# Splitting a sum of squares in high and low halves on VectorE, and two fp32r products in place of one in fp32, in the state-space rounds

## The chip, the cores and the metric

The kernel runs on one core of one Trainium2 chip. The time is that of one execution on the device, in microseconds; a run's time is compared as the median of several. All tensors are fp32 in memory. TensorE multiplies either in fp32 or in fp32r, a format that keeps fewer bits of each number. The kernel makes up for that by splitting operands in a high half (the value rounded to fp32r) and a low half (what is left of it).

## What is computed

Two transformer-like blocks in a row on 256 tokens of width 1024. The change lies in the second block, in its state-space branch (Mamba-2). There, 2048 channels stand in 8 groups of 256, and the result of each group is gated and then normed over the group's 256 channels:

```python
y = ssd_chunked(xh, dt, a, bm, cm)
y = y + d_skip.reshape(SSM_GROUPS, hg)[:, :, None] * xh
y = y.reshape(b, s, SSM_INNER) * jax.nn.silu(z)
yg = y.reshape(b, s, SSM_GROUPS, SSM_INNER // SSM_GROUPS)
yg = yg * lax.rsqrt(jnp.mean(yg * yg, axis=-1, keepdims=True) + RMS_EPS)
y = yg.reshape(b, s, SSM_INNER) * norm_w
```

The sum of `yg * yg` over the 256 channels of a group is what the change computes in another way.

## The kernel before

**Units.** All large products read weights in units of 1024 by 256. SyncE loads a unit into `raw`, ScalarE copies it to fp32r (`split_hi`, line 208, into `w_hi`), VectorE subtracts that from the raw values (`split_lo`, line 214, into `w_lo`), and TensorE makes three products of each 128-row slice (`products`, line 246: high by high, high by low, low by high). There are three slots for units, and a bank of PSUM for each. A slot is filled again once its unit is done; a bank once VectorE or ScalarE has evacuated it.

**Rounds.** The eight groups are worked on in rounds. In round i (1 to 7), TensorE runs the unit `x` of group i, `ssm_scores(i-1)`, the first half of the unit `b_c`, `ssm_sums(i-2)`, the second half, `ssm_values(i-1)` and the unit `z` (lines 2034 to 2043). Each engine has its order written out by hand, and takes its instructions in that order; between engines, semaphores hold them apart.

VectorE in round i (lines 1526 to 1539): `ssm_inputs(i-1)` (lines 1466 and 1468, waits for the scores), a weight split, `ssm_mask(i-1)` (line 1477, waits for ScalarE's decay; `ssm_values(i-1)` on TensorE waits for it), `ssm_scale(i-2)` (line 1509, waits for the norm), `ssm_low(i-2)` (line 999, waits for ScalarE's `ssm_out`), `ssm_skip(i-1)` (1484), an evacuation (989), a weight split, the convolution (1205), a weight split, `ssm_gate(i-1)` (1491 and 1493) and `ssm_pair(i-1)` (1498).

ScalarE in round i (lines 902 to 917): evacuation of `x` (459), a weight copy, four convolution taps (611), a weight copy, the exponents (860), the silu (848), a weight copy, `ssm_square(i-1)` (873), the silu of `z`, the decay (868), `ssm_norm(i-1)` and `ssm_out(i-1)` (lines 449, 450 and 883). The norm waits for TensorE's `ssm_sums(i-1)`, which stands in TensorE's round i+1.

**The sum of squares.** ScalarE squares the gated result of a group, `d_y`, two tiles of 128 channels by 256 tokens, into `d_sq`. VectorE adds the two tiles (`ssm_pair`, line 1498). TensorE multiplies the sum by a matrix of ones in fp32 (`ssm_sums`, line 2024, through the helper `mm`, line 1637), which adds over the 128 partitions. ScalarE turns the result into the inverse root (`ssm_norm`), and VectorE scales `d_y` by it (`ssm_scale`).

**After the rounds** (lines 2045 to 2056): the gate units `ga`. Their first bank is freed by ScalarE's `gate` (line 694), which stands behind `ssm_out(6)` in ScalarE's order. `ssm_pair(7)` and `ssm_sums(7)` lie among these units.

`Chain` (line 86) is a helper: called with an instruction, it lets it raise a semaphore and makes the same engine wait for that before its next instruction. `x_hi` and `x_lo` are the fp32r operand tiles, `OPND` = 40 of them each of 128 by 256; in the rounds the last two are free.

Of the kernel before, what the change touches and what calls it, by code (L numbers as in the profile page):

```python
# [8 lines left out]
FP32 = mybir.dt.float32  # L9
FP32R = mybir.dt.float32r  # L10
ALU = mybir.AluOpType
ACT = mybir.ActivationFunctionType
AXX = mybir.AxisListType.X

P = 128
T = 256
# [43 lines left out]
OPND = 40  # L60
# [37 lines left out]
def build(nc, a, out):  # L98

    ctx = ExitStack()  # L100
    with ctx:
        def sb(name, shape, dt=FP32):
            return ctx.enter_context(nc.sbuf_tensor(name, shape, dt))
# [3 lines left out]
        def S(name):  # L107
            if name not in sems:
                sems[name] = ctx.enter_context(nc.semaphore(name))
            return sems[name]  # L110
# [6 lines left out]
        x_hi = sb("x_hi", [P, OPND, T], FP32R)  # L117
        x_lo = sb("x_lo", [P, OPND, T], FP32R)
# [3 lines left out]
        ident, ones, later = (cst[:, n * P:(n + 1) * P] for n in range(3))  # L122
# [15 lines left out]
        def cells(at, *dims):  # L138
            n = 1
            for d in dims:  # L140
                n *= d
            v = arena[:, at:at + n]
            if len(dims) == 2:
                return v.rearrange("p (a b) -> p a b", a=dims[0])
            if len(dims) == 3:
                return v.rearrange("p (a b c) -> p a b c", a=dims[0], b=dims[1])
            return v

        def bank(b, *dims):
            v = ps[:, b, :]  # L150
            if len(dims) == 3:
                return v[:, 0:dims[0] * dims[1] * dims[2]].rearrange("p (a b c) -> p a b c", a=dims[0], b=dims[1])
            if len(dims) == 2:
                return v[:, 0:dims[0] * dims[1]].rearrange("p (a b) -> p a b", a=dims[0])
            return v[:, 0:dims[0]]
# [8 lines left out]
        def need(eng, name, n):  # L164

            if n > 0:
# [10 lines left out]
        n_hi, n_lo = (v[:, M0:M0 + 3, :].rearrange("p a b -> p (a b)").rearrange("p (h c) -> p h c", h=2)  # L177
                      for v in (x_hi, x_lo))
        ones_r, later_r = (x_hi[:, M0 + 3, n * P:(n + 1) * P] for n in range(2))
        dtc, acs = (small[:, n:n + 64].rearrange("p (t h) -> p t h", t=2) for n in (256, 320))  # L180
        skip = tab[:, 40 * KT:40 * KT + 16]
        dtb, a_log = (tab[0:32, n:n + 1] for n in (40 * KT + 16, 40 * KT + 17))
# [67 lines left out]
        def thin_products(dst, hi, lo, at):  # L250

            for k in range(KT):
                for m, (wt, xt) in enumerate(((hi, x_hi), (hi, x_lo), (lo, x_hi))):
# [25 lines left out]
        d_ab, d_cb, d_xd, d_ec, d_sq, d_r, d_y = (cells(3584, 4, T), cells(4624, 384), cells(5008, 2, T), cells(5520, 4, 384),  # L279
                                                  cells(2576, 2, T), cells(3088, T), cells(7056, 2, T))  # L280
# [34 lines left out]
        def U(stage, i, n=0, per=1):  # L315
            return BASE[stage] + per * i + n
# [125 lines left out]
        def _(act):  # L442
            ahead = iter(range(len(FILLED)))
            chain = Chain(act, S("act_chain"))
            A = nc.scalar.activation
# [6 lines left out]
            def tables():  # L452

                act.preload_act_table_set("natural_log_exp_and_others")  # L454

            def evac(u, dst, func=ACT.Copy):

                finished(act, u)
                A(dst, unit_bank(u), func).then_inc(taken(u), 1)

            def split():

                split_hi(act, next(ahead))
# [374 lines left out]
            def ssm_tap(i):  # L838

                evacuated(act, U("ssm", i, 0, 3))  # L840
                evacuated(act, U("ssm", i, 1, 3))
                need(act, "d_L", i)
                first_tap(d_xp, d_cv, "_2", ssm_tiles(i)).then_inc(S("rnn_c0"), 1)

            def ssm_silu(i):

                act.wait_ge(S("rnn_cv"), i + 5)
                A(d_cv, d_cv, ACT.Silu).then_inc(S("rnn_qk"), 1)  # L848

            def ssm_z(i):  # L850

                evac(U("ssm", i, 2, 3), d_z, ACT.Silu)

            def ssm_exponents(j, heads=range(4)):

                act.wait_ge(S("rnn_bc"), 16 * j + 80)
                act.wait_ge(S("rnn_num"), j + 4)
                for h in heads:
                    for s, (lo, hi, at) in enumerate(((0, T, 0), (P, T, T))):
                        last = A(decay(j)[:, h, at:at + hi - lo], d_ab[:, h, lo:hi], ACT.Relu,  # L860
                                 bias=acs[:, s, 4 * j + h:4 * j + h + 1], scale=-1.0)
                if 3 in heads:
                    last.then_inc(S("rnn_e"), 1)

            def ssm_decay(j):

                act.wait_ge(S("rnn_e"), j + 5)
                A(decay(j), decay(j), ACT.Exp, scale=-1.0).then_inc(S("rnn_w"), 1)

            def ssm_square(j):  # L870

                act.wait_ge(S("rnn_hm"), j + 5)
                A(d_sq, d_y, ACT.Square).then_inc(S("rnn_sq"), 1)

            def ssm_norm(j):

                act.wait_ge(S("rnn_ss"), j + 5)
                inv_rms(d_r, bank(6, T), T).then_inc(S("rnn_r"), 1)

            def ssm_out(j):  # L880

                act.wait_ge(S("rnn_y"), j + 5)
                A(rows(x_hi, 2 * j + YSS, 2), d_y, ACT.Copy).then_inc(S("y_hi"), 1)
# [15 lines left out]
            tables()  # L899
            ssm_decay(0)  # L900

            for i in range(1, 8):
                evac(U("ssm", i, 0, 3), d_xp[:, 0:2, 3:259])
                split()
                ssm_tap(i)
                split()
                ssm_exponents(i)
                ssm_silu(i)
                split()
                ssm_square(i - 1)  # L910
                ssm_z(i)
                tables()
                ssm_decay(i)
                if i == 7:
                    split()
                ssm_norm(i - 1)
                ssm_out(i - 1)
# [58 lines left out]
        def _(dve):  # L976
            ahead = iter(range(len(FILLED)))
            chain = Chain(dve, S("dve_chain"))
            V = nc.vector
            tt, ts, stt = V.tensor_tensor, V.tensor_scalar, V.scalar_tensor_tensor  # L980
# [29 lines left out]
            for b in range(4):  # L1010
                v = slice(2 * b, 2 * b + 2)
# [483 lines left out]
            def ssm_pair(j):  # L1495

                dve.wait_ge(S("rnn_sq"), j + 5)
                tt(d_sq[:, 0], d_sq[:, 0], d_sq[:, 1], ALU.add).then_inc(S("d_pair"), 1)

            def ssm_conv(i):  # L1500

# [120 lines left out]
            for t in range(2):  # L1622
# [3 lines left out]
                for h in range(2):  # L1626
                    v = y_cols(h)
# [5 lines left out]
        def _(pe):  # L1633
            FP, TOK = False, True

            def mm(o, l, r, start=True, stop=True):
                return nc.tensor.matmul(o, l, r, start=start, stop=stop)  # L1637
# [58 lines left out]
            k, q, v = cross_units(0)  # L1696
# [68 lines left out]
            for i in range(1, 5):  # L1765
                k, q, v = (U("cross", i, n, 3) for n in range(3))
# [49 lines left out]
            for i in range(1, 4):  # L1816
                q, k, v = (U("stick", i, n, 3) for n in range(3))
# [36 lines left out]
            q, k, v, o = (U("mlstm", 0, n, 4) for n in range(4))  # L1854
# [8 lines left out]
            for i in range(1, 4):  # L1863
                q, k, v, o = (U("mlstm", i, n, 4) for n in range(4))
# [112 lines left out]
            q, k, v = (U("att", 0, n, 3) for n in range(3))  # L1977
# [8 lines left out]
            for i in (1, 2):  # L1986
                q, k, v = (U("att", i, n, 3) for n in range(3))
# [32 lines left out]

            def ssm_sums(j):

                pe.wait_ge(S("d_pair"), j + 1)
                mm(bank(6, T), ones, d_sq[:, 0]).then_inc(S("rnn_ss"), 1)

            x, b_c, z = (U("ssm", 0, n, 3) for n in range(3))
            att_logits(2)
# [182 lines left out]
```

## Time and profile before

| what | value |
|---|---|
| time, median of 3 runs (range) | 1212.14 us (1210.88 to 1213.48) |
| the profiled execution's own time | 1213.69 us |
| its span | 1211.9 us |
| TensorE busy | 1195.8 us (99%), 9406 products |
| VectorE busy | 819.0 us (68%) |
| ScalarE busy | 672.0 us (55%) |
| mean granted clock of TensorE | 0.996 |

The state-space rounds lie between about 740 and 900 us of the span. Engines are named PE (TensorE products), PEld (TensorE weight loads), DVE (VectorE), ACT (ScalarE). Durations of products overlap, since they are pipelined; their cost is read from one start to the next. An fp32 product is listed as two records.

### The profile page before, as it was taken

The page shows a single profiled execution, that of the slowest core. Times are in us where ns is not written, and L with a number is a line of the kernel's source. Part 1 is how long each engine was busy: PE and PEld are TensorE (multiplying, and loading weights), DVE is VectorE, ACT ScalarE, POOL GpSimd, SP SyncE. Part 2 cuts the span into 40 slices and gives each one's busy share as a digit, 9 for nine tenths or more (in the row PEclk, how much of TensorE's full clock was granted, in tenths as well). Part 3 has the DMA queues.
Part 4 walks back from the last instruction along what each step waited for, and adds up shares of the span by engine and source line. Part 5 has one row for each costly group of instructions (what it writes and reads, how often), then busy time and mean ns, then how long its engine had stood idle before and what let it go on. Part 6 is the DMA issues. An engine that isn't in the chain of part 4 may idle for free.

```text
span 1211.9 us, 21581 instructions
## 1 busy us (share of the span) xinstructions
PE 1195.8 (99%) x9406; PEld 1163.3 (96%) x9406; DVE 819.0 (68%) x928; ACT 672.0 (55%) x802; POOL 11.0 (1%) x24
## 2 busy tenths in 40 slices
PE   9999999999999999999999999999999999999998
PEld 8999999999999999999999998999999998999886
DVE  7866677777655557776547757899985457777543
ACT  7643645676553455544435548889876345555442
POOL 0000000000000000000000000000000000000000
PEclk9999999999999999999999999999999999999999
DMA  9553545555555554556565546556555664455651
GB/s 326 169 162 106 167 146 148 148 150 175 184 194 180 179 168 151 194 184 210 174 206 178 183 133 182 173 160 198 156 164 172 195 208 142 155 174 183 234 191 52
DMA packets 202493, 210.73 MB, mean 174 GB/s; under 512 B 6540, under 2 KB 191244, under 8 KB 202400
## 3 DMA queue, kind: packets, MB, share of 16 engines
q1 hardware_dynamic: 199712, 200.30, 52.1%
q0 software_dynamic: 2112, 8.17, 2.3%
q8 instruction: 74, 1.21, 0.5%
q10 hardware_dynamic: 576, 0.90, 0.2%
q14 instruction: 19, 0.16, 0.0%
HBM read 208.25 MB, written 1.09 MB: 173 GB/s over the span
## 4 chain that ended last, share of the span: by engine, by line
PE 80%; DVE 12%; ACT 5%; issue 1%; DMA 1%; DVEq 0%; ACTq 0%
PE ps L246 64%; PE ps L2128 7%; DVE w_lo L214 5%; PE ps L1637 4%; DVE arena L1205 3%; ACT w_hi L208 2%; PE ps L1686 1%; DVE arena L1477 1%; PE ps L2088 1%; PE ps L1640 1%; DMA arena<-rows 1%; DVE arena L1509 0%; PE ps L254 0%; ACT L454 0%; DMA pcol<-in_params 0%
## 5 line engine op out<-in xcount | busy, mean ns | idle before, releaser
L246 PE MATMUL ps<-x_hi,w_hi 128*128 128x256 f32 x2448 | 701.9, 287 | 1.9 <-ACT arena L694 1.4
L246 PE MATMUL ps<-x_hi,w_lo 128*128 128x256 f32 x2448 | 692.9, 283 | 0.0
L246 PE MATMUL ps<-x_lo,w_hi 128*128 128x256 f32 x2448 | 692.9, 283 | 0.0
L214 DVE TENSOR_TENSOR w_lo<-raw,w_hi 128x2048 fp32r<-128x2048 f32 x187 | 427.5, 2290 | 227.1 <-ACT w_hi L208 227.1
L246 PEld LDWEIGHTS ps<-x_hi,w_hi 128*128 128x128 f32 x2448 | 469.9, 192 | 6.4 <-issue 3.7
L246 PEld LDWEIGHTS ps<-x_lo,w_hi 128*128 128x128 f32 x2448 | 470.0, 192 | 0.7
L246 PEld LDWEIGHTS ps<-x_hi,w_lo 128*128 128x128 f32 x2448 | 469.8, 192 | 0.0
L208 ACT CAST w_hi<-raw 128x2048 fp32r<-128x2048 f32 x187 | 354.3, 1900 | 115.4 <-PE ps L246 71.2
L1637 PE MATMUL ps<-arena 128*128 128x256 f32 (+5 forms) x432 | 66.0, 340 | 0.9 <-ACT arena L848 0.7
L246 PE MATMUL ps<-w_hi,x_hi 128*128 128x256 f32 x224 | 64.3, 287 | 0.0
L246 PE MATMUL ps<-w_lo,x_hi 128*128 128x256 f32 x224 | 63.3, 283 | 0.0
L246 PE MATMUL ps<-w_hi,x_lo 128*128 128x256 f32 x224 | 63.3, 283 | 0.0
L1205 DVE SCALAR_TENSOR_TENSOR arena<-arena,pcol 128x256 f32<-128x256 f32 x144 | 60.1, 480 | 3.5 <-ACT arena L611 2.7
L768 ACT ACTIVATE arena<-ps 128x512 f32<-128x512 f32 x30 | 17.9, 598 | 77.6 <-PE ps L246 77.6
L1637 PEld LDWEIGHTS ps<-arena 128*128 128x128 f32 (+2 forms) x432 | 52.9, 170 | 8.3 <-ACT arena L848 0.9
L2128 PE MATMUL ps<-w_hi,x_hi 128*128 128x512 f32 x128 | 49.8, 389 | 0.0
L2128 PE MATMUL ps<-w_hi,x_lo 128*128 128x512 f32 x128 | 49.8, 389 | 0.0
L2128 PE MATMUL ps<-w_lo,x_hi 128*128 128x512 f32 x128 | 49.8, 389 | 0.0
L1367 DVE TENSOR_TENSOR arena<-arena 128x512 f32<-128x512 f32 x32 | 22.1, 692 | 32.0 <-ACT arena L768 32.0
L246 PEld LDWEIGHTS ps<-w_hi,x_lo 128*128 128x128 f32 x224 | 42.9, 191 | 0.0
L246 PEld LDWEIGHTS ps<-w_hi,x_hi 128*128 128x128 f32 x224 | 42.9, 191 | 0.0
L246 PEld LDWEIGHTS ps<-w_lo,x_hi 128*128 128x128 f32 x224 | 42.9, 191 | 0.0
(237 smaller groups left out, 945.3 us busy)
## 6 DMA issues: line engine op xcount, KB each, us to landing
raw<-in_w_in SPq DMA_DIRECT2D x170, 512.0 KB, 4.7
raw<-in_w_ff SPq DMA_DIRECT2D x64, 512.0 KB, 4.5
raw<-in_w_up SPq DMA_DIRECT2D x32, 512.0 KB, 4.7
raw<-in_w_down SPq DMA_DIRECT2D x32, 512.0 KB, 4.6
raw<-in_w_mem_kv SPq DMA_DIRECT2D x16, 512.0 KB, 6.1
raw<-in_w_out SPq DMA_DIRECT2D x16, 512.0 KB, 4.4
raw<-in_w_ssm_proj SPq DMA_DIRECT2D x16, 512.0 KB, 4.6
raw<-in_w_x_proj SPq DMA_DIRECT2D x8, 512.0 KB, 4.4
```

The lines of the kernel that those rows point to most:

```text
L208: nc.scalar.copy(w_hi[:, s], raw[:, s]).then_inc(S(f"w_hi{s}"), 1)
L214: nc.vector.tensor_tensor(w_lo[:, s], raw[:, s], w_hi[:, s].bitcast(FP32), ALU.subtract)\
L246: last = nc.tensor.matmul(dst, l, r, start=start and k == 0 and m == 0, stop=stop and k == nk - 1 and m == 2)
L768: A(f, unit_bank(u), ACT.Relu).then_inc(taken(u), 1)
L1205: last = stt(dst[:, n], pad[:, n, m:m + T], pc("conv_w" + name, tiles[n] + stride * m), dst[:, n], ALU.mult, ALU.add)
L1367: chain(tt(q, f, bc(rs_row(), 2), ALU.mult))
L1477: tt(decay(j), decay(j), bc(d_cb, 4), ALU.mult).then_inc(S("d_L"), 1)
L1637: return nc.tensor.matmul(o, l, r, start=start, stop=stop)
L1640: return nc.tensor.transpose(o, i, ident[0:i.shape[0], 0:i.shape[0]])
L1686: last = nc.tensor.matmul(dst, l, r, start=kind == 0 and k == 0, stop=kind == 2 and k == KT - 1)
L2088: nc.tensor.matmul(dst, wt[:, u % SLOTS, k, o * P:(o + 1) * P], x_hi[:, H0 + k, :], start=k == 0 and m == 0, stop=False)
L2128: last = nc.tensor.matmul(y_bank(c, t), xt[:, U0 + 4 * (b % 8) + k, t * P:(t + 1) * P], wide(wt[:, u % SLOTS])[:, k], start=b % 8 == 0 and ...
```

## The change

`ssm_pair` on VectorE makes three instructions where it made one: it adds the two squares as before, copies the sum to `d_hi` (fp32r, the tile OPND-2 of `x_hi`), and subtracts that from the sum into `d_lo` (the same tile of `x_lo`). After each of the first two, VectorE waits for the instruction's own semaphore. The semaphore `d_pair` is raised by the last of the three. `ssm_sums` on TensorE makes two fp32r products, ones by `d_hi` and ones by `d_lo`, added in the same bank, in place of the one in fp32. The ones in fp32r are written once by ScalarE into `ones_d` (half of the tile OPND-1 of `x_hi`), after `ssm_decay(0)`, and TensorE waits for that.

```diff
--- before.py
+++ after.py
@@ -177,6 +177,8 @@
         n_hi, n_lo = (v[:, M0:M0 + 3, :].rearrange("p a b -> p (a b)").rearrange("p (h c) -> p h c", h=2)
                       for v in (x_hi, x_lo))
         ones_r, later_r = (x_hi[:, M0 + 3, n * P:(n + 1) * P] for n in range(2))
+        d_hi, d_lo = (v[:, OPND - 2, :] for v in (x_hi, x_lo))
+        ones_d = x_hi[:, OPND - 1, 0:P]
         dtc, acs = (small[:, n:n + 64].rearrange("p (t h) -> p t h", t=2) for n in (256, 320))
         skip = tab[:, 40 * KT:40 * KT + 16]
         dtb, a_log = (tab[0:32, n:n + 1] for n in (40 * KT + 16, 40 * KT + 17))
@@ -899,6 +901,7 @@
             tables()
             ssm_decay(0)
 
+            A(ones_d, ones, ACT.Copy).then_inc(S("ones_d"), 1)
             for i in range(1, 8):
                 evac(U("ssm", i, 0, 3), d_xp[:, 0:2, 3:259])
                 split()
@@ -1495,7 +1498,9 @@
             def ssm_pair(j):
 
                 dve.wait_ge(S("rnn_sq"), j + 5)
-                tt(d_sq[:, 0], d_sq[:, 0], d_sq[:, 1], ALU.add).then_inc(S("d_pair"), 1)
+                chain(tt(d_sq[:, 0], d_sq[:, 0], d_sq[:, 1], ALU.add))
+                chain(V.tensor_copy(d_hi, d_sq[:, 0]))
+                tt(d_lo, d_sq[:, 0], d_hi.bitcast(FP32), ALU.subtract).then_inc(S("d_pair"), 1)
 
             def ssm_conv(i):
 
@@ -2020,8 +2025,10 @@
 
             def ssm_sums(j):
 
+                pe.wait_ge(S("ones_d"), 1)
                 pe.wait_ge(S("d_pair"), j + 1)
-                mm(bank(6, T), ones, d_sq[:, 0]).then_inc(S("rnn_ss"), 1)
+                mm(bank(6, T), ones_d, d_hi, True, False)
+                mm(bank(6, T), ones_d, d_lo, False, True).then_inc(S("rnn_ss"), 1)
 
             x, b_c, z = (U("ssm", 0, n, 3) for n in range(3))
             att_logits(2)
```

## Rows read from the trace of the kernel before

**Rows 1.** Chain that ended last, 740 to 960: start, us, engine, tile, line

```profile
762.70 0.65 PE ps L1637 x4
...
783.54 0.64 ACT arena L873
...
899.01 4.57 PE ps L246 x36
...
915.78 44.27 PE ps L246 x369
```

**Rows 2.** VectorE's timeline, 736 to 930: start, us, line, operation, [idle before, releaser]

```profile
763.83 0.56 DVE L1466 TENSOR_TENSOR arena<-ps,cst 128x384 f32<-128x384 f32 x1 [2.91 <-PE ps L1640]
...
784.21 0.42 DVE L1498 TENSOR_TENSOR arena<-arena 128x256 f32<-128x256 f32 x1 [0.70 <-ACT arena L873]
784.55 0.55 DVE L1466 TENSOR_TENSOR arena<-ps,cst 128x384 f32<-128x384 f32 x1
...
787.88 1.75 DVE L1477 TENSOR_TENSOR arena<-arena 128x1536 f32<-128x1536 f32 x1
...
802.81 0.68 DVE L1491 TENSOR_TENSOR arena<-arena,ps 128x512 f32<-128x512 f32 x1
803.52 0.69 DVE L1493 TENSOR_TENSOR arena<-arena 128x512 f32<-128x512 f32 x1
...
867.02 0.43 DVE L1498 TENSOR_TENSOR arena<-arena 128x256 f32<-128x256 f32 x1 [0.70 <-ACT arena L873]
...
870.70 1.75 DVE L1477 TENSOR_TENSOR arena<-arena 128x1536 f32<-128x1536 f32 x1
...
910.49 2.29 DVE L214 TENSOR_TENSOR w_lo<-raw,w_hi 128x2048 fp32r<-128x2048 f32 x1 [1.37 <-ACT w_hi L208]
```

**Rows 3.** TensorE's timeline in the rounds, same columns

```profile
786.71 0.28 PE L246 MATMUL ps<-x_lo,w_hi 128*128 128x256 f32 x1
786.83 0.28 PE L246 MATMUL ps<-x_hi,w_lo 128*128 128x256 f32 x1
786.96 0.60 PE L1637 MATMUL ps<-arena,cst 128*128 128x256 f32 x2
...
787.51 0.28 PE L246 MATMUL ps<-x_lo,w_hi 128*128 128x256 f32 x1
...
790.34 1.57 PE L1637 MATMUL ps<-arena 128*64 128x256 f32 x16
...
810.80 0.44 PE L1637 MATMUL ps<-arena 128*64 128x256 f32 x2
...
868.88 0.60 PE L1637 MATMUL ps<-arena,cst 128*128 128x256 f32 x2
...
872.50 1.57 PE L1637 MATMUL ps<-arena 128*64 128x256 f32 x16 [0.17 <-DVE arena L1477]
...
899.01 0.39 PE L246 MATMUL ps<-x_hi,w_hi 128*128 128x256 f32 x1 [1.41 <-ACT arena L694]
```

**Rows 4.** ScalarE's timeline, 736 to 930, same columns

```profile
749.06 2.08 ACT L611 ACTIVATE arena<-arena,pcol 128x256 f32<-128x256 f32 x4 [0.80 <-DVE arena L989]
```

**Rows 5.** VectorE's groups by form, 740 to 920: busy us, mean ns | idle before

```profile
L1498 DVE TENSOR_TENSOR arena<-arena 128x256 f32<-128x256 f32 x8 | 3.4, 426 | 5.6 <-ACT arena L873 5.6
...
L1290 DVE COPY mix<-arena 128x512 f32<-128x512 f32 x3 | 1.3, 426 | 0.1
```

**Rows 6.** Stretches: us, busy of PE, PEld, DVE, ACT, POOL, clock, DMA share, GB/s

```profile
748.00:750.00 2.00, 2.00 (x17) 1.41 (x17) 2.00 (x4) 1.20 (x3) 0.00 (x0) 0.70 0.81 281
750.00:752.00 2.00, 2.00 (x10) 2.00 (x10) 2.00 (x4) 2.00 (x4) 0.00 (x0) 0.50 0.00 0
898.00:900.00 2.00, 0.99 (x8) 0.99 (x9) 1.16 (x3) 1.99 (x4) 0.00 (x0) 1.00 1.01 353
```

**Rows 7.** TensorE's timeline behind two long idle stretches

```profile
747.91 2.12 PE L1637 MATMUL ps<-mix,arena 128*64 128x256 f32 x16 [1.91 <-DVE mix L1477]
...
1022.21 0.55 PE L2088 MATMUL ps<-x_hi,w_hi 128*128 128x256 f32 x1 [2.91 <-ACT x_hi L946]
```

## The prediction

> **What bounds the kernel now.** I read the chain of work that ended last, over 740 to 960 us, first. The reader is to see that it leaves TensorE at the scores of the second state-space round (762.70), then names only VectorE and ScalarE pieces until 899.01, and from there on TensorE again [rows 1]. So although TensorE is called busy nearly all the time, in the rounds it isn't what sets the pace.
>
> VectorE's timeline gives that pace [rows 2]. The masks (line 1477) of rounds 3 and 7 start at 787.88 and 870.70: 82.82 us for four rounds, 20.70 each. TensorE's timeline gives its own pace [rows 3]: the values products (sixteen records at 790.34) come again at 810.80, 20.46 us later. TensorE is the faster by 0.24 us a round. In round 3 the mask ends at 789.63, 0.71 before the values start; in round 7 it ends at 872.45 and TensorE starts at 872.50 after an idle that the row puts down to the mask: the lead is used up. At 899.01 TensorE has waited 1.41 us for a bank that ScalarE's first gate frees, and that gate stands behind `ssm_out(6)` and so behind VectorE's last full round.
>
> **The change, part by part.**
>
> TensorE. One fp32 product of 128x256 goes, two fp32r ones come. In the timeline the product before the old one starts at 786.83 and the second one after it at 787.51 [rows 3]: 0.68 us, of which two ordinary steps of 0.12 (786.83 stands 0.12 behind its forerunner, as all fp32r products do) are 0.24, so the old product costs 0.44. Two fp32r products at 0.12 cost 0.24. Gain 0.20 us for each of 8 pairs, 1.6 us in all. But in rounds 2 to 7, and before the wait at 899.01, TensorE only arrives earlier at a wait for somebody else. What lies on the path is the product of pair 7 alone, after 899.01: 0.20 us. The added wait on `ones_d` is long fulfilled.
>
> ScalarE. One copy of ones, 128x128, once, between `ssm_decay(0)` and the evacuation of the next x unit. It is at most as long as the square of four times its width, 0.64 us [rows 1]; the four taps behind it start at 749.06 after 0.80 us idle [rows 4]. That idle hides it: nothing. Without that cover, up to 0.64 once.
>
> VectorE, the part that counts. In each `ssm_pair` two instructions are added, each behind a wait on VectorE's own semaphore. Before, the pair's sum starts at 784.21 and the next instruction at 784.55: 0.34 us, less than the sum's 0.42, since the next one waits for nothing of it and overlaps [rows 2]. Where one VectorE instruction does wait for the one in front (line 1493 behind 1491), it starts 0.03 us behind its end: 802.81 plus 0.68 is 803.49, and it starts at 803.52. So after the change: sum 0.426 [rows 5] plus 0.03, then the copy plus 0.03, then the subtraction, which is of the sum's kind and size and lets its follower overlap, 0.34. The copy from arena to x_hi is not in the trace. The nearest row is a copy in SBUF of twice the width, 128x512, at 426 ns [rows 5]. The 128x256 sum takes the same 426; if a copy moves two elements in the time of one of the sum's, half the width takes off about 0.13, which leaves 0.29. If a copy into fp32r doesn't get that pace, it costs what the sum does, 0.43. I take 0.29, since the row is a copy between SBUF tiles as this is. Added per round: 0.46 plus 0.32, X = 0.78 us; upper bound 0.92.
>
> Where X goes, round by round. Pair 0 is followed by 2.91 us of idle for TensorE's scores (763.83) [rows 2]: hidden. Pairs 1 to 6 have no such idle behind them: their inputs, a weight split and the mask follow back to back, so each pushes the next mask by X and, as the masks hand on to the scaling, ScalarE's output, the next splits, the convolution and the next pair, all that follows. The 0.71 us of lead in round 3 cannot take up 0.78, and later rounds have less. The first gate, and TensorE at 899.01, come 6 X = 4.7 us later. Pair 7 lies behind that; the split behind it (910.49) has waited 1.37 us for ScalarE's weight copy, and X fits there: hidden. Sum so far: 4.7 - 0.2 = 4.5 us.
>
> Who waits for the added instructions directly? TensorE's sum product. In the seventh round the pair starts at 867.02 and the product at 868.88 [rows 2, 3], 1.86 us, against 0.46 + 0.32 + 0.42 = 1.2: the halves are there 0.6 us early.
>
> The granted clock. TensorE reaches the bank wait by values 6, which the mask of round 7 holds up by 5 X = 3.9, less 0.2 for the shorter product: 3.7 later, while the release is 4.7 later. The idle of 1.41 grows to 2.4. After an idle of 1.91 (747.91) the clock was granted at 0.70 and 0.50 in the next two stretches of 2 us, its lower level, which lost 2 x 0.30 + 2 x 0.50 = 1.6 us; after 2.91 (1022.21) a product took 0.55 where they take 0.28; after 1.41 the clock stayed at 1.00 [rows 6, 7]. The new idle lies between the two that were followed by a fall, but 1.91 and 1.41 are close to each other, so I can't call it certain: 0 to 1.6, I take 0.8. The shorter new idles in rounds 4 to 7 (21.48 for VectorE against 20.26 for TensorE: 1.2 us each) are below the 1.41 that left the clock alone.
>
> Total: 4.5 + 0.8 = 5.3 us. The profiled execution took 1213.69 us (span 1211.9), 1.55 above the median 1212.14; on it the sum gives 1219.0, on the median 1217.4, and that is what I forecast.
>
> **A price weighed against a rule.** The row says that a wait on the engine's own semaphore costs the overlap: 0.71 us from start to start with it (802.81 to 803.52, 0.68 long), but 0.34 without for an instruction of 0.42. The Trainium skill, page "VectorE: DVE Perf Modes", section "The DRAIN you can't avoid", says that a semaphore after each instruction costs nothing extra against one at the end. The rows of this case speak against it; it is the third rival below.
>
> **The rivals.**
>
> First, VectorE's added work is absorbed and only TensorE's gain is left. Condition: the rounds have at least 0.78 us of VectorE slack each, or TensorE's own sequence ends last. It would give 8 x 0.20 = 1.6 us off: 1210.5, not slower. For it: VectorE isn't called full in these rounds. Against: all its idle in a round is a hand-over to ScalarE and back, which moves along with it, and TensorE's idle at 872.50 is already put down to the mask. The point from which it decides is a VectorE pace below 20.26 us.
>
> Second, the copy runs at the sum's pace and the clock falls: 6 x 0.92 - 0.2 + 1.6 = 6.9: 1219.0. If waits of TensorE also move in on `d_pair` (0.6 us of slack, less 0.13), there may be another microsecond or two: 1221.
>
> Third, the waits don't cost the overlap: X = 0.34 + (0.29 - 0.08) = 0.55, six of them 3.3, less 0.2: 3.1 without a fall of the clock, 1215.2; 1216.8 with one.
>
> Fourth, the change doesn't do what it says: an fp32r pair behind another kind of product costs as much as the fp32 one. That takes away the 0.2 on the path and 1.2 us more of idle elsewhere goes; 1217.6, not to be told from the forecast in time, only in the rows.
>
> **How the numbers follow.** Forecast (VectorE's pace carries X six times, clock fallen or not, fourth rival within it): 0.70, from 1216.6 (no fall) to 1219.0. Second, beyond 1219.0: 0.08. Third: 0.10. First: 0.08. The rest, 0.04, is something between the first and the third, of which half the sign of a gain: TensorE's 1.6 together with a fall of the clock that doesn't happen. The range leaves out the first rival and the end of the second: 1214.4 to 1220.6. About 0.2% (2.4 us) is what a measurement of this kernel can tell from no change. The first rival's 1.6 lies within it. Slower by more: 0.88; within: 0.10; faster by more: 0.02.
>
> **What would show each step.** In the profile of the changed kernel: the masks stand 21.4 to 21.6 us apart from round 3 on; three VectorE instructions in each pair, 0.46 and 0.32 apart, the copy at 0.29 (0.43: second rival); sum products as two steps of 0.12; TensorE idle about 0.5 us before the values of round 3 and 1.2 in rounds 4 to 7, put down to the mask; 2.4 us before the products that follow the first gate; the stretch from there to the end as long as before but for 0.2 us and the clock. The prediction is wrong if the masks keep 20.7 us, if the chain stays on TensorE through the rounds, or if TensorE waits for `d_pair`.

## The result, and the profile after

| | before | after |
|---|---|---|
| median of 11 executions each (range) | 1213.21 us (1210.58 to 1213.73) | 1216.59 us (1214.96 to 1218.04) |
| profiled execution's own time, and its span | 1213.69 us, 1211.9 us | 1216.59 us, 1214.8 us |
| mean granted clock of the profiled execution | 0.996 | 0.998 |
| VectorE busy | 819.0 us | 825.0 us |
| TensorE busy | 1195.8 us | 1193.3 us |

The kernel after is slower: ratio 1.0033, with a 95% interval of 1.0025 to 1.0041. The forecast was 1217.4 us, in a range of 1214.4 to 1220.6.

The executions of one kernel fall into groups by TensorE's mean granted clock, and the groups stand about 1.5 us apart. Over all comparisons before stood at 1210.6 us with a mean clock of 0.999, at 1212.0 with 0.998, at 1213.5 with 0.996 or 0.997. Medians move with the mix of these groups (before's went from 1212.0 to 1213.2 in different comparisons), so small differences are read below at equal clock too. After against before, at equal clock: 1214.99 against 1210.55 (0.999, two executions of after), 1216.63 against 1212.00 (0.998, eight of them). That is 4.4 and 4.6 us, against the 4.5 of the sum without its clock term.

VectorE's timeline of the kernel after (start, us, line, operation, idle before and its releaser) has the pair's three instructions where one stood in [rows 2]. The first group of lines is pair 0, the second pair 1, the third pair 7:

```profile
759.94 0.42 DVE L1501 TENSOR_TENSOR arena<-arena 128x256 f32<-128x256 f32 x1 [0.70 <-ACT arena L875]
760.40 0.29 DVE L1502 CAST x_hi<-arena 128x256 fp32r<-128x256 f32 x1
760.72 0.43 DVE L1503 TENSOR_TENSOR x_lo<-arena,x_hi 128x256 fp32r<-128x256 f32 x1
763.27 0.56 DVE L1469 TENSOR_TENSOR arena<-ps,cst 128x384 f32<-128x384 f32 x1 [2.12 <-PE ps L1645]
...
766.60 1.75 DVE L1480 TENSOR_TENSOR arena<-arena 128x1536 f32<-128x1536 f32 x1
...
783.64 0.43 DVE L1501 TENSOR_TENSOR arena<-arena 128x256 f32<-128x256 f32 x1 [0.70 <-ACT arena L875]
784.10 0.29 DVE L1502 CAST x_hi<-arena 128x256 fp32r<-128x256 f32 x1
784.42 0.43 DVE L1503 TENSOR_TENSOR x_lo<-arena,x_hi 128x256 fp32r<-128x256 f32 x1
784.76 0.55 DVE L1469 TENSOR_TENSOR arena<-ps,cst 128x384 f32<-128x384 f32 x1
...
788.10 1.75 DVE L1480 TENSOR_TENSOR arena<-arena 128x1536 f32<-128x1536 f32 x1
...
913.69 0.42 DVE L1503 TENSOR_TENSOR x_lo<-arena,x_hi 128x256 fp32r<-128x256 f32 x1
914.70 2.29 DVE L216 TENSOR_TENSOR w_lo<-raw,w_hi 128x2048 fp32r<-128x2048 f32 x1 [0.59 <-ACT w_hi L210]
```

From the sum to the next inputs it is now 0.46 + 0.32 + 0.34 = 1.12 us, where [rows 2] had 0.34: X is 0.78. The masks (L1480) stand 21.50 us apart, 766.60 to 788.10, against 20.70. Pair 0 only shortens an idle, 2.91 to 2.12, and so does pair 7, 1.37 to 0.59.

TensorE's timeline of the kernel after, in the rounds and at the first gate, beside [rows 3]:

```profile
765.93 0.28 PE L1642 MATMUL ps<-x_hi 128*128 128x256 f32 x1
766.05 0.28 PE L1642 MATMUL ps<-x_lo,x_hi 128*128 128x256 f32 x1
...
789.90 1.57 PE L1642 MATMUL ps<-arena 128*64 128x256 f32 x16 [0.41 <-DVE arena L1480]
...
811.40 1.57 PE L1642 MATMUL ps<-arena 128*64 128x256 f32 x16 [1.14 <-DVE arena L1480]
...
892.13 0.28 PE L248 MATMUL ps<-x_hi,w_lo 128*128 128x256 f32 x1
892.49 0.36 PE L1642 MATMUL ps<-x_hi 128*128 128x256 f32 x1
...
895.82 0.35 PE L248 MATMUL ps<-x_hi,w_hi 128*128 128x256 f32 x1 [0.71 <-DVE w_lo L216]
...
903.21 0.39 PE L248 MATMUL ps<-x_hi,w_hi 128*128 128x256 f32 x1 [1.40 <-ACT arena L696]
...
1026.24 0.36 PE L2095 MATMUL ps<-x_hi,w_hi 128*128 128x256 f32 x1 [2.91 <-ACT x_hi L949]
```

TensorE is faster by the two short products and spends the gain waiting for the mask: 0.41 us in round 3, 1.14 or 1.15 in each of rounds 4 to 7. The view of TensorE's waits (total us, times, longest) has that in one line, here of before and then of after:

```profile
PE ps L1637 <- DVE arena L1477: 0.2, 1, 0.2
PE ps L1642 <- DVE arena L1480: 5.0, 5, 1.2
```

Where the time came from: the first mask of this stretch is 0.56 us earlier than before (another wait, not of the change); from there to the first gate it is 4.76 us more, six rounds of 0.8; pair 7 gives 0.2 back. So TensorE is 4.0 us late at the long idle (1026.24 against 1022.21). From there to TensorE's last product, the kernel after makes up 1.3 us (1206.15 in before, 1208.85 in after), because of the clock behind that idle, and the profiled span is only 2.9 us longer. The view by stretches (us, busy of PE, PEld, VectorE, ScalarE, POOL, clock, DMA share, GB/s) of before:

```profile
1022.00:1024.00 2.00, 1.79 (x8) 1.82 (x9) 2.00 (x6) 1.50 (x4) 0.00 (x0) 0.50 0.69 242
1024.00:1026.00 2.00, 2.00 (x14) 2.00 (x13) 2.00 (x7) 1.54 (x3) 0.00 (x0) 0.68 0.00 0
```

and of after, which was granted the full clock (2.4 GHz) there (the second line), and around the first gate as well (the first line):

```profile
900.00:904.00 4.00, 2.60 (x22) 2.39 (x21) 2.42 (x6) 3.60 (x5) 0.00 (x0) 1.00 0.84 264
1024.00:1028.00 4.00, 1.76 (x15) 1.79 (x16) 3.61 (x10) 2.24 (x5) 0.00 (x0) 1.00 0.80 262
```

The same idle of 2.91 us was followed by the lower level (1.2 GHz) in one execution and not in the other. In the profiled executions of all kernels here the clock fell, before 1200 us, only at two places, behind the idles of 1.91 and 2.91 us of [rows 7]. After, e9_both_after and e10_four_after had a fall at one of them and have a mean clock of 0.998; ten others had one at both and have 0.996 or 0.997; e7_ends had one fall, about twice as long, and has 0.997. So kernels at equal mean clock are, nearly, kernels with as many falls.

### The profile page after: what moved, and what is told of

The parts are those of the page before. It is cut to its first block, busy times and chain, and to the rows that moved or that the text cites. A ratio compares the mean times of both kernels' runs of the same rounds, so it can differ in the third digit from the quotient of the medians.

```text
span 1214.8 us, 21606 instructions
## 1 busy us (share of the span) xinstructions
PE 1193.3 (98%) x9406; PEld 1160.8 (96%) x9406; DVE 825.0 (68%) x944; ACT 672.8 (55%) x803; POOL 11.0 (1%) x24
## 4 chain that ended last, share of the span: by engine, by line
PE 79%; DVE 12%; ACT 5%; issue 2%; DMA 1%; DVEq 0%; ACTq 0%
PE ps L248 64%; PE ps L2135 7%; PE ps L1642 4%; DVE w_lo L216 4%; DVE arena L1208 3%; ACT w_hi L210 2%; PE ps L1691 1%; DVE arena L1480 1%; PE ps L1645 1%; PE ps L2095 1%; DMA arena<-rows 1%; DVE arena L1514 0%; PE ps L256 0%; DMA pcol<-in_params 0%; ACT L456 0%
```

## The experiments

Each ran beside before on one chip. Masks and waits are from its profiled execution; "0.998" is its mean over the executions with that mean granted clock (before 1212.0, after 1216.63). These are two executions for e3_unwaited and e4_twice, three for e7_ends and e12_gate_after, four to eight for the others, and within such a group they differ by up to 0.8 us. In the code cuts "..." stands for lines left out.

| kernel | median | ratio (95%) | 0.998 | masks apart | TensorE's idle before values |
|---|---|---|---|---|---|
| e1_dve_only | 1216.68 | 1.0039 (1.0026 to 1.0053) | 1216.66 | 21.50 | 0.96 |
| e2_no_low | 1211.63 | 0.9992 (0.9983 to 1.0000) | 1211.83 | 20.71 | 0.48 |
| e3_unwaited | 1215.88 | 1.0028 (1.0016 to 1.0040) | 1215.15 | 21.24 | 0.7 |
| e4_twice | 1222.06 | 1.0080 (1.0065 to 1.0095) | 1221.32 | 22.28 | 1.6 |
| e7_ends | 1211.99 | 0.9999 (0.9988 to 1.0010) | 1211.81 | 20.71 | 0.17 in rounds 6 and 7 |
| e5_later_before | 1211.01 | 0.9994 (0.9985 to 1.0003) | 1210.76 | 20.46 | none |
| e6_later_after | 1212.92 | 1.0010 (1.0001 to 1.0019) | 1212.92 | 20.70 | 0.35 |
| e9_both_after | 1213.19 | 1.0011 (1.0003 to 1.0020) | 1213.07 | 20.70 | 0.35 |
| e10_four_after | 1210.74 | 0.9991 (0.9983 to 1.0000) | 1210.62 | 20.67 | 0.32 |
| e11_four_before | 1209.65 | 0.9973 (0.9963 to 0.9983) | 1209.77 | 20.46 | none |
| e12_gate_after | 1209.60 | 0.9974 (0.9963 to 0.9984) | 1208.45 | 20.28 | none |
| e13_gate_before | 1209.90 | 0.9983 (0.9974 to 0.9992) | 1209.83 | 20.46 | none |

**VectorE's part alone.** The halves are made on VectorE, and TensorE keeps the fp32 product.

```diff
-                mm(bank(6, T), ones_d, d_hi, True, False)
-                mm(bank(6, T), ones_d, d_lo, False, True).then_inc(S("rnn_ss"), 1)
+                mm(bank(6, T), ones, d_sq[:, 0]).then_inc(S("rnn_ss"), 1)
```

> The split into halves on VectorE as in the change, but TensorE keeps the one fp32 product of the unsplit sum. If VectorE's pace carries the added time (theory), the masks stand 21.48 us apart and the time is 4.7 us above before, 0.2 above the changed kernel. If the loss came from the new products on TensorE, this kernel is within 1 us of before.

At equal clock it takes 1216.66 us, after 1216.63. The masks are 21.5 apart as in after, and TensorE's idle before each values product is 0.96 us instead of 1.15: the shorter products of rounds 2 to 7 buy idle, nothing else. The 0.2 us of pair 7's product shows in the trace only: from the first gate to the long idle's end TensorE takes 123.21 us here, 123.20 in before and 123.03 in after. The whole loss is VectorE's.

**TensorE's part alone.** The low half is left out, so the sum is that of the rounded values; VectorE makes one instruction as before.

```diff
-                chain(tt(d_sq[:, 0], d_sq[:, 0], d_sq[:, 1], ALU.add))
-                chain(V.tensor_copy(d_hi, d_sq[:, 0]))
-                tt(d_lo, d_sq[:, 0], d_hi.bitcast(FP32), ALU.subtract).then_inc(S("d_pair"), 1)
+                tt(d_hi, d_sq[:, 0], d_sq[:, 1], ALU.add).then_inc(S("d_pair"), 1)
...
-                mm(bank(6, T), ones_d, d_hi, True, False)
-                mm(bank(6, T), ones_d, d_lo, False, True).then_inc(S("rnn_ss"), 1)
+                mm(bank(6, T), ones_d, d_hi).then_inc(S("rnn_ss"), 1)
```

> The low half is left out of the sum: VectorE's one addition writes its result in fp32r, and TensorE makes one fp32r product in place of the fp32 one. VectorE's work is that of before, TensorE's is 0.32 us shorter a pair. Theory (VectorE's pace of 20.70 us sets the rounds): only the product behind the first gate counts, 0.2 to 0.4 us below before. Rival (TensorE sets the time): 8 x 0.32 = 2.6 us below before.

Eight products that are 0.32 us shorter, 2.6 us of TensorE, gave 0.2 us at one clock (1211.83 against 1212.0) and 0.4 at the other (1210.14 against 1210.55). The masks keep 20.71, and TensorE waits for them:

```profile
830.99 1.35 PE L1640 MATMUL ps<-arena 128*64 128x256 f32 x12 [0.48 <-DVE arena L1480]
```

**Without the two waits.** Copy and subtraction work on other data that is long there, with no wait in front, and the fp32 product stays on TensorE. The halves are not used.

```diff
+                tt(d_sq[:, 0], d_sq[:, 0], d_sq[:, 1], ALU.add).then_inc(S("d_pair"), 1)
+                V.tensor_copy(d_hi, d_y[:, 0])
+                tt(d_lo, d_y[:, 0], d_y[:, 1], ALU.subtract)
...
+                mm(bank(6, T), ones, d_sq[:, 0]).then_inc(S("rnn_ss"), 1)
```

> The pair's sum as before with the fp32 product, and behind it a copy and a subtraction of the same sizes on other data, for which nothing waits and which wait for nothing. Theory (an own-semaphore wait costs the overlap of 0.09 and a gap of 0.03 us): each round 0.55 us longer than before, masks 21.25 apart, 3.3 us above before. Rival (the waits cost nothing): masks 21.48 apart and 4.7 us above before, as in the kernel with the split on VectorE alone.

VectorE's timeline of this kernel:

```profile
826.86 0.29 DVE L1502 CAST x_hi<-arena 128x256 fp32r<-128x256 f32 x1
827.06 0.42 DVE L1503 TENSOR_TENSOR x_lo<-arena 128x256 fp32r<-128x256 f32 x1
827.40 0.55 DVE L1469 TENSOR_TENSOR arena<-ps,cst 128x384 f32<-128x384 f32 x1
```

Without a wait behind it the copy takes 0.20 from start to start instead of 0.32, and the masks stand 21.24 apart instead of 21.50. Each wait on VectorE's own semaphore costs 0.12 to 0.13 us a round. The two together are 6 x 0.26 = 1.6 us by the masks, and 1.5 us of the kernel (1215.15, from two executions, against 1216.66 at equal clock).

**Copy and subtraction twice.**

```diff
+                for _ in range(2):
+                    chain(V.tensor_copy(d_hi, d_sq[:, 0]))
+                    last = tt(d_lo, d_sq[:, 0], d_hi.bitcast(FP32), ALU.subtract)
+                    if _ == 0:
+                        chain(last)
+                last.then_inc(S("d_pair"), 1)
```

> The changed kernel with copy and subtraction made twice, each waited for: VectorE gets 0.32 + 0.46 = 0.78 us more in each pair. Theory: masks 22.26 us apart, another 4.7 us: 9.2 above before. The idle of TensorE before the values grows to about 1.9 us, as long as the one that was followed by a fall of the granted clock; a fall inside a round is mostly hidden. Rival (the added time is partly absorbed): less than 7 above before.

The second dose costs the same as the first: masks 22.28 apart, 0.78 more than after, and 4.7 us at equal clock (1221.32 against 1216.63), which is six times 0.78. Here TensorE does wait for the halves. The view names the wait in two rounds:

```profile
875.07 0.36 PE L1646 MATMUL ps<-x_hi 128*128 128x256 f32 x1 [0.15 <-DVE x_lo L1504]
...
897.34 0.36 PE L1646 MATMUL ps<-x_hi 128*128 128x256 f32 x1 [0.86 <-DVE x_lo L1504]
```

In the three rounds before, the product starts 0.42 or 0.43 us behind its forerunner instead of 0.12, which is the same wait, too short to be listed. None of these waits moves the end: TensorE's work behind the first gate starts 7.62 us behind the last mask's start here (908.06 against 900.44), and 7.61 or 7.62 in before and after too. They do take from the idle before the values, which the expectation had at 1.9 us and which is 1.55 to 1.57. No fall of the clock followed it in any of the four rounds.

**The change for pairs 0 and 7 alone.**

```diff
+                if j in (0, 7):
                     chain(tt(d_sq[:, 0], d_sq[:, 0], d_sq[:, 1], ALU.add))
                     chain(V.tensor_copy(d_hi, d_sq[:, 0]))
                     tt(d_lo, d_sq[:, 0], d_hi.bitcast(FP32), ALU.subtract).then_inc(S("d_pair"), 1)
+                else:
+                    tt(d_sq[:, 0], d_sq[:, 0], d_sq[:, 1], ALU.add).then_inc(S("d_pair"), 1)
...
+                    mm(bank(6, T), ones, d_sq[:, 0]).then_inc(S("rnn_ss"), 1)
```

> The change made for pairs 0 and 7 alone, the other six as before. Theory: the 0.78 us on VectorE are hidden at pair 0 (2.91 us idle behind it) and at pair 7 (1.37 us), and the product of pair 7 brings 0.2: 0.2 below before. Rival (each added split costs its time wherever it stands): 1.4 above before.

1211.81 against 1212.0 at equal clock, ratio 0.9999: the same three instructions cost nothing where 2.91 and 1.37 us of idle stand behind them. The 0.2 us of pair 7's product is in the trace: 123.03 us from the first gate to the long idle's end (897.26 to 1020.29), against 123.20 in before. The cost of pairs 1 to 6 is one of their place.

**The pair behind the next inputs.** Before and after with the pair moved from in front of the next `ssm_inputs` to behind it, so that the scores are taken up first.

```diff
                 ssm_inputs(i - 1)
+                if i > 1:
+                    ssm_pair(i - 2)
                 split()
                 ssm_mask(i - 1)
...
                 ssm_gate(i - 1)
-                ssm_pair(i - 1)
...
             ssm_inputs(7)
+            ssm_pair(6)
```

> The kernel before, with the pair's sum put behind the next round's inputs on VectorE, so that ScalarE's squaring no longer leaves VectorE idle for 0.70 us. Theory: VectorE's pace falls to 20.0 us, below TensorE's 20.46, the rounds go by TensorE and its idle at the values of rounds 6 and 7 and at the first gate (0.08 + 0.24 + 0.10 + 1.41 = 1.8 us) goes: 1.8 below before. Rival (TensorE already sets the time): same as before.

> The same move of the pair, now three instructions, in the changed kernel. Theory: VectorE's pace is 21.48 - 0.70 = 20.78 us, still above TensorE's 20.26, so VectorE sets the rounds: 6 x 0.08 - 0.2 = 0.3 above before, and 4.2 below the changed kernel. If what costs is anything else than VectorE's time in the rounds, it stays 4 us above before.

Both came out 0.6 us too high at equal clock (1.2 below before instead of 1.8, and 0.9 above instead of 0.3). With the move, before runs at TensorE's pace (20.46) and after at 20.70, near the 20.78 expected. What both expectations left out is pair 0. In its old place it lay in the idle of 2.91 us; behind the inputs it lies between the scores and the mask. VectorE's timeline of e6_later_after:

```profile
763.39 0.56 DVE L1469 TENSOR_TENSOR arena<-ps,cst 128x384 f32<-128x384 f32 x1 [4.08 <-PE ps L1647]
...
767.85 1.75 DVE L1480 TENSOR_TENSOR arena<-arena 128x1536 f32<-128x1536 f32 x1
```

From the start of the inputs to the mask this is 4.46 us, where before has 3.33 (763.83 to 767.16): 1.1 us once, which is nearly all that e6_later_after is above before in the trace between the first mask and the first gate (154.06 against 152.91). In e5_later_before the same stretch takes 3.67, 0.3 more. The idle at the first gate did not vanish either. It went from 1.41 to 0.85 in the one and from 1.40 to 1.2 in the other; ScalarE's first gate still follows the last mask (7.62 and 7.61 us from the mask's start to TensorE's start). In the kernel with the halves TensorE also waits for the last pair, which has moved back, without moving that start:

```profile
890.10 0.36 PE L1644 MATMUL ps<-x_hi 128*128 128x256 f32 x1 [0.42 <-DVE x_lo L1503]
```

**An evacuation sooner.** To shorten VectorE's part between the mask and its own next split, the evacuation of `b_c` goes in front of `ssm_low`, on top of the move above (ScalarE's taps get a wait for `ssm_skip` with it).

```diff
                     ssm_scale(i - 2)
+                evac(U("ssm", i, 1, 3), d_xp[:, 2:4, 3:259])
+                if i > 1:
                     ssm_low(i - 2)
                 ssm_skip(i - 1)
-                evac(U("ssm", i, 1, 3), d_xp[:, 2:4, 3:259])
```

> The changed kernel with the pair behind the next inputs and the evacuation of b_c moved in front of ssm_low, where VectorE was idle for 0.70 us (ScalarE's taps wait for ssm_skip in its place). Theory: VectorE's pace is 21.48 - 0.70 - 0.60 = 20.2 us, just under TensorE's 20.26; the rounds go by TensorE, and now its 0.20 us a pair count: 1.8 + 1.6 = 3.4 below before. Rival (TensorE's saving never counts): 1.8 below before or less.

A clear miss, 1.0 us above before at equal clock instead of 3.4 below: the masks stay 20.70 apart, and pair 0 again lies behind the inputs. VectorE's timeline of this kernel, and ScalarE's:

```profile
790.15 0.87 DVE L1515 SCALAR_TENSOR_TENSOR arena<-arena,pcol 128x256 f32<-128x256 f32 x2
...
794.00 2.29 DVE L216 TENSOR_TENSOR w_lo<-raw,w_hi 128x2048 fp32r<-128x2048 f32 x1 [0.93 <-ACT w_hi L210]
```

```profile
791.06 0.63 ACT L886 ACTIVATE x_hi<-arena 128x512 fp32r<-128x512 f32 x1 [2.18 <-DVE arena L1515]
791.60 0.58 ACT L461 ACTIVATE arena<-ps 128x512 f32<-128x512 f32 x1
792.08 1.89 ACT L210 CAST w_hi<-raw 128x2048 fp32r<-128x2048 f32 x1
```

VectorE's split waits for ScalarE's weight copy, which stands behind `ssm_out` (L886), which has waited 2.18 us for VectorE's scaling (L1515). The loop goes through both engines, and a shorter piece on one of them only lengthens its wait for the other.

**Four moves.** So both orders are changed, in before and in after: the two moves above (the pair for 1 to 5 only, so that pair 0 keeps its cover), ScalarE's `ssm_out` put behind the next evacuation and weight copy, and `ssm_scale(6)` put in front of a split. ScalarE's part of the last two, and then VectorE's:

```diff
                 split()
+                if i > 1:
+                    ssm_out(i - 2)
                 ssm_tap(i)
...
                 ssm_norm(i - 1)
-                ssm_out(i - 1)
+            ssm_out(6)
```

```diff
             ssm_mask(7)
+            ssm_scale(6)
             split()
-            ssm_scale(6)
```

> The changed kernel with four moves: pairs 1 to 5 behind the next inputs; the evacuation of b_c in front of ssm_low; on ScalarE the next x unit's evacuation and weight copy in front of ssm_out, so that VectorE's next split no longer waits for them; behind the rounds ssm_scale(6) in front of a split. Theory: no engine but TensorE sets the pace, masks 20.26 us apart, TensorE idles neither at the values nor at the first gate: 1.8 + 8 x 0.20 = 3.4 below before, 1.6 below the same four moves without the change. Rival (TensorE's saving never counts, the split always costs): not below the kernel with the four moves alone.

> The kernel before with the same four moves. Theory: masks 20.46 us apart, and the 1.8 us of TensorE's idle at the values of rounds 6 and 7 and at the first gate are gone: 1.8 below before. Rival (the idle at the first gate has another cause than the place of ssm_scale(6) and ssm_out(6)): 0.9 below before or less, as with the later pair alone.

The idle at the first gate is gone in both. e11_four_before is 2.3 us below before at equal clock, where 1.8 was expected, and e10_four_after 1.4 instead of 3.4; the interval of its median's ratio still touches 1. But the kernel with the halves is not the lower of the two; it is 0.85 us above (1210.62 against 1209.77 at equal clock) where it should have been 1.6 below. VectorE's timeline of e10_four_after, with TensorE's line for the values of the round before behind it:

```profile
864.97 0.56 DVE L1472 TENSOR_TENSOR arena<-ps,cst 128x384 f32<-128x384 f32 x1 [0.77 <-PE ps L1652]
865.45 0.74 DVE L1474 TENSOR_TENSOR arena<-ps,small 128x256 f32<-128x256 f32 x2
866.11 0.41 DVE L1504 TENSOR_TENSOR arena<-arena 128x256 f32<-128x256 f32 x1
866.56 0.29 DVE L1505 CAST x_hi<-arena 128x256 fp32r<-128x256 f32 x1
866.89 0.42 DVE L1506 TENSOR_TENSOR x_lo<-arena,x_hi 128x256 fp32r<-128x256 f32 x1
867.23 2.29 DVE L216 TENSOR_TENSOR w_lo<-raw,w_hi 128x2048 fp32r<-128x2048 f32 x1
869.43 1.75 DVE L1483 TENSOR_TENSOR arena<-arena 128x1536 f32<-128x1536 f32 x1
```

```profile
850.57 1.57 PE L1649 MATMUL ps<-arena 128*64 128x256 f32 x16 [0.32 <-DVE arena L1483]
```

The pair's 1.12 us still lie between the scores and the mask, only behind the inputs instead of in front of them. From the start of the inputs to the mask it is 4.46 us here and 3.67 in e11_four_before (845.23 to 848.90). A loop of two engines is left: values, unit `z`, unit `x` and scores on TensorE, then inputs, pair, split and mask on VectorE, and the values again. It takes 20.67 us, 0.4 more than TensorE's own work with the short products.

**The gate in front of a split.** That reading was put to a test. The pair can't simply come sooner: it waits for ScalarE's square, which stands behind a weight copy, after VectorE's gate, which stands behind a split. So gate and square go in front of split and copy, the pair goes back to its old place, and the other three moves stay. VectorE's part, and then ScalarE's:

```diff
                 ssm_conv(i)
-                split()
                 ssm_gate(i - 1)
+                split()
                 ssm_pair(i - 1)
```

```diff
-                split()
                 ssm_square(i - 1)
+                split()
                 ssm_z(i)
```

> The kernel after, with three of the four moves (the evacuation of b_c, ScalarE's chain out, the scale of round 6), the pair left in its place in front of the next inputs, and in each round the gate of VectorE and the square of ScalarE put in front of a weight split instead of behind it. In e10_four_after the masks are 20.67 us apart and TensorE waits 0.32 us for each, because the sum, the copy and the subtraction (1.12 us) stand between the scores and the mask. Theory: with the square done before the split ends, the pair starts as the split ends (about 0.6 us sooner than in its old place) and delays the next inputs by some 0.35 us instead of 1.12, so the mask comes early enough and TensorE sets the pace at 20.26 us: six rounds of 0.41 and 0.8 once at the first round less than e10_four_after, some 1208 us in the median, about 1.5 us below e13_gate_before. Rival: TensorE is then made to wait by the later split (it ends 1.4 us later) or by ScalarE, masks 20.6 or more apart, and the time is 1210.5 or above, no lower than e13_gate_before.

> The kernel before with the same moves as e12_gate_after. In e11_four_before the masks are already 20.46 us apart, TensorE's own pace, so theory: no more than that, 1209.6 us in the median, masks 20.46 apart; then the eight cheaper products of the change (0.2 us each) show for the first time as the difference to e12_gate_after. Rival: the later split or ScalarE makes TensorE wait, 1210.5 us or more.

VectorE's timeline of e12_gate_after:

```profile
863.90 0.42 DVE L1504 TENSOR_TENSOR arena<-arena 128x256 f32<-128x256 f32 x1
864.35 0.29 DVE L1505 CAST x_hi<-arena 128x256 fp32r<-128x256 f32 x1
864.68 0.43 DVE L1506 TENSOR_TENSOR x_lo<-arena,x_hi 128x256 fp32r<-128x256 f32 x1
865.20 0.56 DVE L1472 TENSOR_TENSOR arena<-ps,cst 128x384 f32<-128x384 f32 x1
...
866.34 2.28 DVE L216 TENSOR_TENSOR w_lo<-raw,w_hi 128x2048 fp32r<-128x2048 f32 x1
```

The pair starts as the split ends, and the 0.70 us of waiting for ScalarE in front of it are gone. The inputs start 0.52 us behind the subtraction's start, where they take 0.34 when they only wait for their turn (784.42 to 784.76 in after): so the pair is now done before the scores are. The masks stand 20.28 apart (848.25 to 868.53), against 20.46 in e13_gate_before. TensorE has no idle left before the values in either. At equal clock the change is now a gain, for the first time: 1208.45 against 1209.83 us (0.998), 1206.83 against 1208.26 (0.999) and 1209.78 against 1211.27 (0.996 and 0.997), 1.4 to 1.5 us, near the 1.6 of eight products. The medians, 1209.60 and 1209.90, hardly show it, because 6 of e12_gate_after's 11 executions ran with a mean clock of 0.996 or 0.997 and only 3 of e13_gate_before's 11. Whether that comes with the kernel or by chance is open. The profiled execution of e12_gate_after had falls behind the idles at 747 and 1018 us, the same two that are followed by one in [rows 7]. The best versions, by median, are e12_gate_after and e11_four_before, equal within their intervals, with ratios of 0.9974 and 0.9973; at equal clock e12_gate_after is the lower by 1.3 us (1208.45 against 1209.77).

## Why the prediction was right, and where not

**The bound.** Right. From the second round on the pace is a loop over VectorE and ScalarE. e1_dve_only and e2_no_low show it from both sides: VectorE's part alone costs all that the change costs, and 2.6 us off TensorE alone give 0.2 to 0.4.

**X.** Right in size and in its parts: 0.46, 0.32 and 0.34 measured, 0.78 added, the copy at 0.29 as estimated from the copy of twice the width [rows 5]. Of it, 0.12 to 0.13 for each wait is shown by e3_unwaited, so the third rival (waits that cost no overlap, 1215.2) is out. The Trainium skill, page "VectorE: DVE Perf Modes", section "The DRAIN you can't avoid", says that a semaphore after each instruction costs nothing extra, from a run of eight copies. This case's traces don't agree for an instruction that waits for the one in front: the wait cost 0.12 to 0.13 us. Whether raising a semaphore without such a wait is free was not tested.

**Six times X.** Right: 4.76 us in the trace against 4.7, and pairs 0 and 7 are hidden, which e7_ends shows by itself. TensorE's idle before the values, 0.41 in round 3 and 1.15 behind it, is close to the 0.5 and 1.2 that were named. The first rival fails in its condition: the loop has no slack of 0.78 for pairs 1 to 6.

**TensorE's products.** Right: two steps of 0.12 where one of 0.44 was. The fourth rival is out by these rows; in e12_gate_after against e13_gate_before the eight of them are worth 1.4 us.

**The halves in time.** Right for seven pairs of eight, wrong for pair 6. The slack of 0.6 us was read from pair 5. Pair 6 has less: in before its sum starts at 887.73 and the product at 888.86, 1.13 us, under the 1.2 that the three instructions need. In after the subtraction ends at 892.35 and the product starts at 892.49, 0.36 behind its forerunner instead of 0.12. So TensorE did wait for `d_pair`, which the prediction names as a sign of being wrong, by some 0.24 us. It cost nothing, since TensorE's next wait, for the split at 895.82, ends where VectorE lets it.

**The clock term, 0.8 us.** Wrong. The step that failed is "the idle of 1.41 grows to 2.4". It took the bank as the only thing that TensorE would wait for there. There was another: the split of the next unit stands behind the last inputs on VectorE, so it comes late by all six X, as the bank does. TensorE waited for that split 0.71 us at 895.82, then worked, and met the bank 1.40 us too early, as before [rows 3]. The trace of before has the wait already, too short to be listed: VectorE's split ends at 891.48, and TensorE's next product starts 0.31 us behind its forerunner instead of 0.12. TensorE's two rows and VectorE's row, of before:

```profile
891.31 0.28 PE L246 MATMUL ps<-x_hi,w_lo 128*128 128x256 f32 x1
891.62 0.35 PE L246 MATMUL ps<-x_hi,w_hi 128*128 128x256 f32 x1
```

```profile
889.20 2.28 DVE L214 TENSOR_TENSOR w_lo<-raw,w_hi 128x2048 fp32r<-128x2048 f32 x1
```

In after that split starts at 893.39 and ends at 895.67, and the product starts at 895.82, 0.15 behind it, where before has 0.14. From that product to the one behind the bank wait it is 7.39 us in both (891.62 to 899.01, 895.82 to 903.21), so the idle at the bank could not grow. The idle was cut in two, neither half was followed by a lower clock, and the delay of the end was the same. So the forecast's 5.3 has a part too much, and 4.5 holds at equal clock. In the median the two kernels are 3.4 us apart, since six of before's eleven executions there took 1213.2 us or more, as those with a clock of 0.996 or 0.997 do, and eight of after's ran at 0.998. That the forecast of 1217.4 lies only 0.8 above the measured median, just this term, is in part luck: the starting value 1212.14 happens to be one of before at 0.998, and after's median is one at 0.998 too.

**The median of before.** The working took 1212.14 from three executions. With more of them it was between 1212.0 and 1213.2, by the mix of clocks. This is as large as several of the terms that were summed, and the forecast did not say so.

## What to carry to other kernels

Before giving work to an engine that is busy 68% of the time, look for the place of the work: the same three instructions cost nothing at two places and 0.78 us at six others. Products saved on the engine that is busy 99% were worth 0.2 to 0.4 us of 2.6 as long as its idle was put down to the other one. Before moving a piece, see what covers it where it stands: pair 0 cost nothing in its old place and 1.1 us behind the inputs. And look for waits too short to be listed, by a step that is longer than the ordinary one. Where a loop runs over two engines, follow it through both orders before moving one piece; after e9_both_after's miss, what helped was to put the loop's steps in front of prefetch work (weight splits and copies) on both engines at once, and only then did the change itself pay.

## What the runs showed of the hardware

A wait of VectorE for the instruction in front of it costs 0.12 to 0.13 us at 128x256, twice over: 0.46 against 0.34 for a sum, 0.32 against 0.20 for a copy. A copy from fp32 to fp32r within SBUF takes 0.29 us at 128x256, where a sum of the same size takes 0.42.

The lower clock does not follow an idle each time. The same idle of 2.91 us was followed by 0.50 and 0.68 in the profiled execution of before and by 1.00 in that of after. Over the fourteen profiled executions, the idle of 1.91 to 1.93 us before the values of round 1 was followed by a fall in twelve and not in e7_ends and e10_four_after, and the idle of 2.90 or 2.91 us before line 2088 of before, and the same products of the others, in twelve and not in after and e9_both_after. The four idles of 1.55 to 1.57 us in e4_twice and the idle of 1.40 at the first gate were never followed by one. The executions of one kernel group by mean clock some 1.5 us apart, near the 1.6 us that one such fall was worth in [rows 6]. What decides it in a given execution is open.
